# A union of edits to a one-core, three-layer kernel: order of the modulation units, steps of the side work, expert weights in halves, the logits' operands and the start of the second block

## The reference, cut to what matters

```python
mod = jax.nn.silu(c) @ w_ada[l] + b_ada[l]                  # 12 units of 512 columns
sh1, sc1, g1, sh2, sc2, g2 = jnp.split(mod, 6, axis=-1)
h = modulate(x, norm1_g[l], sh1, sc1)                       # rms_norm * (1 + scale) + shift
q_a, k_a, v_a, qk_m, v_m, o_m, gates = jnp.split(h @ w_in[l], offs, axis=-1)
...                                                          # attention and mLSTM side by side
x = x + g1 * (concat([attn, hm]) @ w_out[l])
h2 = modulate(x, norm2_g[l], sh2, sc2)
x = x + g2 * hier_moe(h2, ...)   # 32 experts, two for each token: (silu(x w1) * (x w3)) w2
```

## Time and profile before

| | us |
|---|---|
| median of 3 runs | 1373.76 (1370.18 to 1374.32) |
| the profiled execution | 1369.11 |
| its span, first to last instruction | 1367.3 |
| TensorE busy | 1153.6 (84%) |
| VectorE / ScalarE busy | 610.4 / 543.0 |
| mean granted TensorE clock | 0.944 |

### The profile page before, as it was taken

One profiled execution on the slowest core, in us unless ns is written; L12 is line 12 of the kernel. 1 busy time (PEld: TensorE's weight loads), 2 busy tenths in 40 slices (PEclk: granted clock), 3 DMA queues, 4 the chain that ended last, 5 costly groups with the idle time before them and its releaser, 6 DMA issues.

```text
span 1367.3 us, 22377 instructions
## 1 busy us (share of the span) xinstructions
PE 1153.6 (84%) x9627; PEld 916.5 (67%) x9627; DVE 610.4 (45%) x1359; ACT 543.0 (40%) x1211; POOL 0.2 (0%) x4
## 2 busy tenths in 40 slices
PE   6989988857566666656589989999999989999997
PEld 4867677534243433424256768899998758899997
DVE  4564664201110110111065766665555865655554
ACT  4554554211100110110154665555554754655553
POOL 0000000000000000000000000000000000000000
PEclk9999998988887889988899999999999999999999
DMA  9896847899999999999978655644546665655520
GB/s 389 344 351 236 349 198 275 343 426 428 427 426 428 424 426 427 427 427 427 428 301 322 225 189 224 263 181 178 182 141 231 235 239 185 247 185 186 185 93 32
DMA packets 29569, 397.53 MB, mean 291 GB/s; under 512 B 3480, under 2 KB 4888, under 8 KB 5400
## 3 DMA queue, kind: packets, MB, share of 16 engines
q1 hardware_dynamic: 29032, 395.72, 72.6%
q10 hardware_dynamic: 432, 0.30, 0.1%
HBM read 394.97 MB, written 1.05 MB: 290 GB/s over the span
## 4 chain that ended last, share of the span: by engine, by line
PE 61%; DMA 20%; DVE 10%; ACT 7%; issue 2%; SPq 0%; ACTq 0%; DVEq 0%
PE ps L141 61%; DMA mem<-in_w 13%; DMA ring<-in_w 5%; DVE mem L141 5%; DVE memr L141 3%; ACT mem L141 3%; ACT memr L141 3%; DVE small L141 1%; DMA ring<-in_wpk 1%; DMA posi<-in_pos 1%; ACT L141 0%; ACT rowb L141 0%; DVE x L141 0%; SPq L141 0%; DVE mcol L141 0%
## 5 line engine op out<-in xcount | busy, mean ns | idle before, releaser
L141 PE MATMUL ps<-memr 128*128 128x256 f32 (+1 forms) x4680 | 669.4, 302 | 15.2 <-DVE memr L141 15.1
L141 PEld LDWEIGHTS ps<-memr 128*128 128x128 f32 x4680 | 611.0, 192 | 60.3 <-DVE memr L141 25.4
L141 DVE TENSOR_TENSOR memr<-ring,memr 128x512 fp32r<-128x512 f32 x440 | 297.1, 690 | 239.3 <-ACT memr L141 235.9
L141 PE MATMUL ps<-mem 128*32 128x256 f32 (+5 forms) x2360 | 301.8, 423 | 85.8 <-DMA ring<-in_w 34.0
L141 ACT ACTIVATE memr<-ring 128x512 fp32r<-128x512 f32 x440 | 267.2, 626 | 213.9 <-PE ps L141 206.7
L141 PEld LDWEIGHTS ps<-mem 128*32 128x32 f32 (+3 forms) x2360 | 186.9, 150 | 158.7 <-issue 106.7
L141 ACT ACTIVATE mem<-ps 128x256 f32<-128x256 f32 (+5 forms) x307 | 121.3, 407 | 415.0 <-PE ps L141 414.1
L141 PE MATMUL ps<-ring,mem 128*32 128x256 f32 x1408 | 151.5, 430 | 39.6 <-DMA mem<-in_w 34.7
L141 DVE TENSOR_TENSOR mem<-mem,ps 128x256 f32<-128x256 f32 (+1 forms) x76 | 31.7, 418 | 271.2 <-ACT mem L141 271.2
L141 PEld LDWEIGHTS ps<-ring,mem 128*32 128x32 f32 x1408 | 72.9, 123 | 78.8 <-issue 53.1
L141 DVE COPY mem<-ps 32x256 f32<-32x256 f32 (+2 forms) x81 | 38.2, 471 | 120.0 <-PE ps L141 119.0
(11 more groups left out here) (91 smaller groups left out, 380.5 us busy)
## 6 DMA issues: line engine op xcount, KB each, us to landing
ring<-in_wpk SPq DMA_DIRECT2D x89, 2048.0 KB, 8.0
mem<-in_w SPq DMA_DIRECT2D x52, 2048.0 KB, 34.3
ring<-in_w SPq DMA_DIRECT2D x44, 2048.0 KB, 36.4
mem<-in_wpk SPq DMA_DIRECT2D x1, 2048.0 KB, 10.4
ring<-in_wpk SPq DMA_DIRECT2D x2, 1024.0 KB, 5.1
x<-in_x SPq DMA_DIRECT2D x2, 512.0 KB, 5.6
out_dram<-mem SPq DMA_DIRECT2D x4, 256.0 KB, 2.4
cst<-in_cst SPq DMA_DIRECT2D x1, 944.0 KB
```

The source lines that it names most:

```text
L141: ins = o[1](*o[2], **o[3])
```

## The change

Seven edits. (1) Modulation unit 4 is loaded ahead of the second projection's unit, and its matmuls run inside `first_half`, behind the transposes and ahead of the fifth slab; its copy out of PSUM comes at chunk 7. Units 5 to 9 of the modulation move up one place likewise, in the list of loads and in the program. (2) `step_side` advances the side work after five of the modulation units as well; `work` goes on to the next generator in the same step when one ends, and `conv` has one step less. (3) The weights `w1` and `w3` are stored as two units that hold half of the rows of both (`w13a`, `w13b`); an expert's 32 matmuls take first the one, then the other, and each is released after its 16. (4) The last expert's `w2` is loaded by two DMAs, the second half issued first. (5) The logits' operands are swapped: 8 matmuls with the 40 columns as the stationary operand, a VectorE copy and two small transposes, which stand behind the first four of the 16 transposes of `hT`. (6) At the seam each sum is added as soon as its bank is done, the first four ahead of the norm, whose squares 0 to 3 no longer wait for the last scatter. (7) Two slabs of the second block's first projection are staged behind the first square.

```diff
-      mixed(ada(0, 0), ada(0, 2), (U_IN + 3, 8), ada(0, 1), ada(0, 3), (U_IN + 4, 8), ada(0, 4), (U_IN + 6, 8), ada(0, 5),
-            ada(0, 6), (U_IN + 5, 8), ada(0, 7), ada(0, 8), (U_IN, 8), ada(0, 9), ada(0, 10), (U_IN + 1, 8), ada(0, 11),
+      mixed(ada(0, 0), ada(0, 2), (U_IN + 3, 8), ada(0, 1), ada(0, 3), ada(0, 4), (U_IN + 4, 8), ada(0, 5), (U_IN + 6, 8),
+            ada(0, 6), ada(0, 7), (U_IN + 5, 8), ada(0, 8), ada(0, 9), (U_IN, 8), ada(0, 10), (U_IN + 1, 8), ada(0, 11),
...
-            for name in ("w1", "w3", "w2"):
+            for name in ("w13a", "w13b", "w2"):
...                                           # in load_unit
+            w = units[n].shape[1]
+            if n == moe_last - 1:
+                w = w // 2
+                last_half.append(S.dma(s_half, slots[slot][:, w:2 * w], units[n][:, w:2 * w], after=after))
+                after = []
+            state["recs"][n] = S.dma(ringsem[slot], slots[slot][:, 0:w], units[n][:, 0:w], after=after)
...                                           # in slab_done
-            for g in list(side):
-                if next(g, StopIteration) is StopIteration:
-                    side.remove(g)
+            step_side()
...                                           # in first_half
             ada_close(True)
+            ada_mm(0, 4)
...                                           # in conv
             first(4 * u)
-            yield
...
-        modulate_x(0, 0, rB_r, x_r, {4: first_half}, recs=h2_r)
+        modulate_x(0, 0, rB_r, x_r, {4: first_half, 7: ada_copy}, recs=h2_r)
...                                           # in work
-                g, n = jobs[0]
-                for _ in range(n):
-                    if next(g, StopIteration) is StopIteration:
-                        jobs.pop(0)
-                        break
-                yield
+                if next(jobs[0], StopIteration) is StopIteration:
+                    jobs.pop(0)
+                else:
+                    yield
...
-        ada_unit(0, 4)
+        ada_unit(0, 5)
+        step_side()
         bk, r = project_T(h2, h2_r, 256, 128)
...
-        ada_unit(0, 5)
         ada_unit(0, 6)
+        step_side()
+        ada_unit(0, 7)
+        step_side()
         vm_r += project(h2, h2_r, ...)
-        ada_unit(0, 7)
         ada_unit(0, 8)
+        step_side()
+        ada_unit(0, 9)
         drain()
...
         rope_unit(qst, qT, qt_r, 0.125)
-        ada_unit(0, 9)
         ada_unit(0, 10)
...                                           # the logits
-            for tt in range(2):
-                r = mm(ps[:, 40 * tt:40 * tt + 40], hT[:, k, 128 * tt:128 * tt + 128], w40[:, k, :], k == 0 and tt == 0,
-                       k == 7 and tt == 1, after=fr + [h_r[k], ld_rows])
+            r = mm(ps[0:40, 0:256], w40[:, k, :], hT[:, k, :], k == 0, k == 7, after=fr + [h_r[k], ld_rows])
+        lgT = sq[0:40, 0, :]
+        lgT_r = V(vt.tensor_copy, lgT, ps[0:40, 0:256], after=[r] + sq_free[0])
...                                           # behind the first four transposes of hT
+                    for t_ in range(2):
+                        r = T(te.transpose, ps[:, 40 * t_:40 * t_ + 40], lgT[:, 128 * t_:128 * t_ + 128],
+                              cst[0:40, K_ID:K_ID + 40], after=fr + [lgT_r])
...                                           # in group
-                w1u, l1 = unit("cols")
-                w3u, l3 = unit("cols")
-                for k in range(8):
-                    for j in range(4):
-                        w = (w1u, w3u)[j // 2]
-                        r = mm(..., w[:, k, 256 * (j % 2):256 * (j % 2) + 256], k == 0, k == 7, after=fr + [l1, l3, xgr[g][k]])
-                release(r)
-                release(r)
+                for half in range(2):
+                    w13, ld = unit("rows")
+                    for k in range(4 * half, 4 * half + 4):
+                        for j in range(4):
+                            r = mm(..., w13[:, k % 4, 256 * j:256 * j + 256], k == 0, k == 7, after=fr + [ld, xgr[g][k]])
+                    release(r)
...                                           # the matmuls of w2
+                               after=fr + [a, l2] + (last_half if e == 31 and kx >= 2 else []))
...                                           # the seam
+        def add_experts(n):
+            x1_r[n] = V(vt.scalar_tensor_tensor, out=xT[:, n, :], ..., after=[acc_r[n // 2], ada_rec[(0, 10 + n // 4)]])
+        for n in range(4):
+            add_experts(n)
         for n in range(8):
-            x1_r[n] = V(vt.scalar_tensor_tensor, ..., after=[acc_r[3], ada_rec[(0, 10 + n // 4)]])
-            sq_r[n] = A(sc.activation, sqX[:, n, :], xT[:, n, :], ACT.Square, after=[x1_r[n]] + moe_r)
+            if n >= 4:
+                add_experts(n)
+            sq_r[n] = A(sc.activation, sqX[:, n, :], xT[:, n, :], ACT.Square,
+                        after=[x1_r[n]] + (moe_r if n >= 4 else []))
+            if n == 0:
+                st["hold"] = False
+                stage(2)
+                st["hold"] = True
```

More of the change, by code:

```diff
@@ L294, in load_unit @@
             state["load"] += 1
-            state["recs"][n] = S.dma(ringsem[slot], slots[slot][:, 0:units[n].shape[1]], units[n], after=after)
+            w = units[n].shape[1]
[4 more added lines that the diff above has]
+            state["recs"][n] = S.dma(ringsem[slot], slots[slot][:, 0:w], units[n][:, 0:w], after=after)
             state["slot"][n] = slot
@@ L350, in slab_done, with step_side @@
             stage()
-            for g in list(side):
-                if next(g, StopIteration) is StopIteration:
-                    side.remove(g)
+            step_side()
+        def step_side(n=1):
+            for _ in range(n):
+                for g in list(side):
+                    if next(g, StopIteration) is StopIteration:
+                        side.remove(g)
         for slot in range(RING):
@@ L1081, in work @@
             while jobs:
-                g, n = jobs[0]
-                for _ in range(n):
-                    if next(g, StopIteration) is StopIteration:
-                        jobs.pop(0)
-                        break
-                yield
+                if next(jobs[0], StopIteration) is StopIteration:
+                    jobs.pop(0)
+                else:
+                    yield
         gate_weights()
-        jobs += [(conv(0, copies), 1)]
+        jobs.append(conv(0, copies))
         side.append(work())
@@ L1093, in program @@
         copies = conv_copy(1, bk, r)
-        jobs += [(conv(1, copies), 1), (gate_rows(*gates()), 1)]
+        jobs += [conv(1, copies), gate_rows(*gates())]
         if not side:
             side.append(work())
-        ada_unit(0, 4)
+        ada_unit(0, 5)
+        step_side()
         bk, r = project_T(h2, h2_r, 256, 128)
@@ L1182, in program @@
         for k in range(8):
-            for tt in range(2):
-                r = mm(ps[:, 40 * tt:40 * tt + 40], hT[:, k, 128 * tt:128 * tt + 128], w40[:, k, :], k == 0 and tt == 0,
-                       k == 7 and tt == 1, after=fr + [h_r[k], ld_rows])
-        lg_r = V(vt.tensor_tensor, lg, ps[:, 0:80].rearrange("p (t n) -> p t n", t=2),
-                 bc(rows[:, R_BR:R_BR + 40], [128, 2, 40], 1), ALU.add, after=[r, ld_rows])
-        PB.give(b, [lg_r])
+            r = mm(ps[0:40, 0:256], w40[:, k, :], hT[:, k, :], k == 0, k == 7, after=fr + [h_r[k], ld_rows])
+        lgT = sq[0:40, 0, :]
+        lgT_r = V(vt.tensor_copy, lgT, ps[0:40, 0:256], after=[r] + sq_free[0])
+        PB.give(b, [lgT_r])
+        lg_r = None
         xr = []
@@ L1196, in program @@
                 PB.give(b, [xr[-1]])
-        hT_last = r
+                hT_last = r
+                if lg_r is None:
+                    b, ps, fr = PB.take()
+                    for t_ in range(2):
+                        r = T(te.transpose, ps[:, 40 * t_:40 * t_ + 40], lgT[:, 128 * t_:128 * t_ + 128],
+                              cst[0:40, K_ID:K_ID + 40], after=fr + [lgT_r])
+                    lg_r = V(vt.tensor_tensor, lg, ps[:, 0:80].rearrange("p (t n) -> p t n", t=2),
+                             bc(rows[:, R_BR:R_BR + 40], [128, 2, 40], 1), ALU.add, after=[r, ld_rows])
+                    PB.give(b, [lg_r])
         load_unit(RING + 4, [hT_last])
@@ L1417, in group @@
                         r = mm(ps[32 * j:32 * j + 32, 0:256], hTe[:, e % 2, kx % 2, 32 * (kx // 2):32 * (kx // 2) + 32],
-                               w2u[:, kx, 256 * j:256 * j + 256], kx == 0, kx == 3, after=fr + [a, l2])
+                               w2u[:, kx, 256 * j:256 * j + 256], kx == 0, kx == 3,
+                               after=fr + [a, l2] + (last_half if e == 31 and kx >= 2 else []))
                 release(r)
@@ L1504, in program @@
                 nst = 0
[L1505 to L1517, removed]
+                for k in range(8):
+                    ld = Rec(s_ext, 16, True)
+                    S.wait(hx_free)
```

(21 more changed lines are left out.)

9 lines of the change are left out of this document (6 added, 3 removed).

## The result

| | before | after |
|---|---|---|
| median, us (4 runs each) | 1373.66 (1370.18 to 1374.32) | 1357.87 (1356.06 to 1359.53) |
| profiled execution, us | 1369.11 | 1357.3 |
| its span, us | 1367.3 | 1355.5 |
| mean granted TensorE clock | 0.944 | 0.949 |

The ratio is 0.9897 with a 95% interval from 0.9881 to 0.9912: faster by 1.0%, some 14 us. 1363.2 us was forecast, a gain of 10.6 us; the two profiled spans differ by 11.8. The direction and the places were right, and the gain was larger than the sum.

What follows compares the result with a forecast made beforehand. TensorE's order and waits bound the front, expert bytes by DMA the middle, TensorE the rest. Terms: -7.2 + 1.6 - 1.85 - 0.9 - 2.3 = -10.6 us, from 1373.8 to 1363.2 us; range 1356 to 1370.

Steps and rivals of the forecast that it cites:

- front: Up to the logits: modulation unit moved, side work advanced earlier; -1.9 - 1.7 + 2.4 - 6.0 = -7.2 us.
- logits: Swapped logits operands: bias at 233.2 us instead of 231.59, the clock still falling midway; +1.6 us.
- first release: First expert's slot comes free after half its 32 matmuls, ahead of the DMA-bound stretch; -1.85 us.
- last expert: At the last expert only 16 matmuls remain when the last half lands; -0.9 us taken, between -3.1 and +2.8.
- seam: Between the blocks: norm right behind the scatter -1.0, slab subtractions moved ahead -1.4, taken as -2.3 us; bounds 0 and -2.4.
- the middle of three: Last expert's tail: upper clock -3.1; second half and w2 at lower clock -0.9 (taken); scatter low too +2.8 us.
- T + 0.4: Last expert's w2 matmuls start 0.4 us behind T, the landing of its w2, if the second half runs low.
- The sign that was wrong: Hole in the DMA share ahead of the experts, 244.4 to 247.9 us before: claimed 1.9 us shorter.
- The kind clock: Rival, chance 0.16: clock doesn't fall ahead of the logits nor at the tail; -2.6 and -2.2 more, 1358.4 us.
- The hole ahead of mLSTM: Rival, chance 0.13: a late transfer or new wait holds the side work, hole stays; 6.0 us less gain, 1369.2 us.
- the gain was carried: Contrary rival, chance 0.07: experts' stream starts no earlier, only the block boundary and tail count; 1370.6 us.
- TensorE didn't become its bound: Contrary rival, chance 0.04: waits at each half keep experts' TensorE at the lower clock; 1 us per expert gives 1391 us.

Runs made afterwards that it cites:

- logits alone: Kernel before with only the logits' operands swapped (40 columns stationary, a copy, two small transposes): 1373.59 us, ratio 1.0005.
- halves alone: Kernel before with only the expert weights w1 and w3 stored as two halves of the rows, each released after its matmuls: 1367.38 us, ratio 0.9967.
- the union: The changed kernel with all seven edits, against the kernel before: 1357.87 us, ratio 0.9897.
- the kernel without the split: The changed kernel with the last expert's w2 loaded in one DMA again: 1358.74 us, ratio 0.9898 to the kernel before.
- without the new logits: The changed kernel with the activations as the stationary operand again: 1357.21 us, ratio 0.9894 to the kernel before.
- late constants: The changed kernel with the old logits and five late loads issued behind the second projection's weights: 1358.20 us, ratio 0.9905 to the kernel before.
- the new order alone: Kernel before with only modulation unit 4 moved ahead and later units one place up: 1372.40 us, ratio 1.0004.
- the steps alone: Kernel before with the side work also advanced behind four modulation units, old order kept: 1366.98 us, ratio 0.9969.

## Why the prediction was right, and by how much it was off

The terms beside what the runs measured, in us. "Trace" is one execution against one: the two that were profiled of the kernels before and after, but for the logits and the first release, which share a stage, those of logits alone and of halves alone against the kernel before. "Executions" is the difference of the means over all profiled executions with and without that edit (front 4 and 5, logits 3 and 3, first release 3 and 7, last expert 6 and 8, seam 6 and 8). "Alone" is the ratio of that group of edits by itself, times 1372:

| step | forecast | trace | executions | alone |
|---|---|---|---|---|
| front (edits 1 and 2) | -7.2 | -6.7 | -6.6 | -8.0 |
| logits | +1.6 | +2.0 | +0.8 | +0.7 |
| first release | -1.85 | -1.6 | -1.5 | } -4.5 |
| last expert | -0.9 | -2.9 | -2.0 | } |
| seam | -2.3 | -2.5 | -2.5 | -1.8 |
| sum | -10.65 | -11.7 | -11.8 | -13.6 |

In the union, release and logits together move the last landing by +0.4 (6.70 us earlier at the logits, 6.29 at the landing). The seam is the one term that no execution's clock touches: from the scatter's start to the fifth slab's subtraction it is 19.36 to 19.38 us in all eight executions without the edit and 16.87 to 16.89 in all six with it. That the sum comes within 1.1 us of the spans is in part luck: the front, and the logits with the release, fell 0.5 and 0.6 us short, and that took back half of what the last expert gave beyond its term.

**The step that was mis-sized is the last expert.** The prediction took -0.9, the middle of three, on the ground that the stretch before runs at the lower clock and so the `w2` matmuls would take twice 1.97 us. Its start was right: T + 0.4 was forecast, and 675.36 is T + 0.39. But the matmuls took 1.97 us, at the upper clock, and the term is -2.9; in the three executions in which they ran low they started at T + 0.1, took 3.2 us, and it is -1.9. The prediction gave the second half and `w2` the same clock, both upper or both lower; the runs show the lower one mostly on one of the two, and that is what the middle case had wrong. The lower end of the bounds, -3.1, was nearly met and the upper, +2.8, was not approached.

The rule of the Trainium skill weighed there (TensorE: Matmul & The Clock Gate, section HAM oscillation — how this bites in real kernels: all matmuls of a block in a row before the next wait for a transfer) would, as the prediction applied it, have made this edit a loss at the tail. The runs show no such loss: the edit alone has the ratio 0.9967 (0.9954 to 0.9980), and the scatter was at the upper clock in every execution. They don't test the rule in the case that this section of the Trainium skill describes, where each wait for a transfer is longer than the matmuls of the block before it: here the halves cut one wait of 5.71 us ahead of the last expert's 32 matmuls into waits of 1.42 and 2.97. The weights come at the pace of the DMA either way; what the halves change is how much work is left when the last bytes land.

**The front** came out as worked out, step by step: no hole at 97 us, no lower clock at either place, one modulation unit fewer at 115 us, a wait ahead of the second projection that was 1.70 us where 2.4 were forecast (0.95 to 2.15 in the four executions with both edits). That the wait would sometimes lower the clock in its turn was named as a bound; it happened in the kernel that has edits 1 and 2 alone, where the 36 matmuls behind it take 6.07 us instead of 4.58:

```profile
48.23 6.07 PE L141 MATMUL ps<-memr 128*128 128x256 f32 x36 [2.15 <-DVE memr L141]
```

What the sum of the front hid is that its parts aren't terms: by the times edit 1 alone is worth 0, and about 3 us once edit 2 is there. The first release came 6.5 us earlier (246.93 to 240.40), where some 7.5 were forecast.

**The logits**: the bias comes at 225.69, 6.21 us behind the start where before it came 5.41 behind it (+0.8), not +1.6; but the first position matmuls behind it then ran at the lower clock (2.23 us, for 1.27 before), so the stage lost about what was forecast. The prediction let 8 of the 16 records pass before the clock falls; it fell 0.14 us behind their start. That the forecast was met is luck of this execution: where the clock didn't fall behind the 1.98 us, in the kernel without the split, the stage was 1.7 us shorter.

**The sign that was wrong** is the hole in the DMA share: forecast 1.9 us shorter, it is 2.7 longer. Its end came 6.5 us earlier as it should, its beginning 9 us earlier. As the prediction held, only the end counts: the stream from the first release to the last landing is as long as before.

**The rivals.** The kind clock came true by half in the execution profiled: kind at the tail, not at the logits. That the median is nearest to its 1358.4 us is luck: of the 5.3 us between the forecast and the median the terms make 1.2, and 4.1 are the offset between profiled and timed executions (below). The hole ahead of mLSTM didn't come back; the gain was carried; the experts' stretch stays at a DMA share of 1.01 and 426 GB/s, so TensorE didn't become its bound.

**From the trace to the times.** The sum was right against the profiled span within 1.1 us, yet the ratio says 14 and the medians 15.8. The kernel before ran between 1368.9 and 1375.9 us in the runs timed beside the experiments, and its profiled execution, 1369.1, lies at the low end; that of after lies 0.6 below its median. The prediction carried the offset of 4.65 us over to the kernel after, and it wasn't carried. The groups measured alone, which don't go through one execution, add up to 13.6. Why executions of the kernel before are slower by some 3 us than the two that were profiled isn't settled: stretches of lower clock that come and go (last section) would do it, but the timed executions left no trace.

No kernel tried beats the union: without the new logits, and with late constants as well, the times lie within each other's intervals.

## What to carry to other kernels

Before adding up edits to one stretch, ask whether one fills a hole whose length goes to the next wait: by the times, the new order alone was worth nothing, and some 3 us once the second hole had been closed. Where a stage is bound by DMA and followed by one bound by TensorE, cut the last units so that little work is left when the last bytes land, and cost that end at the clock of both levels. Where the clock falls in some executions and not in others, one profile gives a term only within 1 to 2 us; set the sum against several timed runs.

## What the hardware showed that was not expected

The same program has its lower clock at different places in different executions. Of the kernel with the steps alone, 168 matmuls behind 2.33 us of idle time took 20.30 and 21.73 us, and the stretch from 215 to 245 us had a mean clock of 0.83 and 0.72. The `w2` matmuls of the last expert took 1.97 or some 3.2 us in kernels with the halves. From the end of the last `w2` matmul to the end of the span the steps alone took 681.5 us in the first execution and 680.0 in the second; the first has a stretch of lower clock there that the second has not, 3.4 us at half the clock and so worth up to 1.7 (columns as in the earlier trace rows):

```profile
803.00:806.40 3.40, 3.40 (x18) 0.79 (x20) 0.52 (x2) 1.77 (x8) 0.00 (x0) 0.51 0.01 2
```

In the two profiled executions of before and after, each with 3.4 to 3.5 us of lower clock in it, the swapped logits, 16 records of 256 columns, took 5.33 us, as long as the 32 of 40 columns before (5.37): halving the number of matmuls bought nothing there. With the clock at 1.00 the 16 took 3.65. The old form took 5.09 to 7.05 us in ten executions, each with some lower clock in it, so how the two compare at the upper clock isn't shown.
